# Filler products in two TensorE gaps of a router, fused attention logits, and a causal block left out

## The chip, the cores and the metric

The kernel runs on one core of a Trainium2 chip. The metric is device time in microseconds (us) of one execution, from start to end. TensorE (PE) does matrix products and transposes, VectorE (DVE) elementwise work and reductions, ScalarE (ACT) activations and copies, GpSimd (POOL) elementwise work in SBUF, and SyncE (SP) issues nearly all DMAs.

## The reference

A transformer stack on 256 tokens of width 1024, fp32 in and out. First a block with an indexed sparse attention, a spatial gating unit and a mixture of experts; then a two-layer stack with a windowed attention and a memory cross attention (layer 0), a gated linear recurrence with the same cross attention (layer 1) and a convolutional feed-forward in each. What the change touches:

```python
def dsa_attention(q, k, v, qi, ki, wi):          # 8 heads of 128
    ...                                           # 64 keys of each query are kept by an index score
    valid = sel <= qpos[None, :, None]            # causal
    logits = einsum('bqhd,bqkhd->bhqk', qb, kg) * (HEAD_DIM ** -0.5)
    logits = where(valid[:, None], logits, -inf)
    p = softmax(logits); out = p @ vg
...
def window_gqa_sink(q, k, v, sink):               # 16 heads of 64, keys within 128 positions
    m = maximum(max(s), sk)
    p = exp(s - m)
    p = p / (sum(p) + exp(sk - m))                # sk: one learned "sink" logit a head
...
def hier_moe(xn, ...):                            # 256 tokens, 4 groups of 8 experts
    g_sel = argmax(g_logits); top_v, top_i = top_k(e_in_group, 2)
    ...                                           # SwiGLU experts 1024 -> 2 x 256 -> 1024
```

## The kernel before, in words

Five engine programs are written out by hand and meet only through semaphores; each engine runs its program in order, so the order in the code is the order of the work. There is no scheduler.

**Linear layers.** Each weight matrix comes from HBM through a ring of SBUF slots, which SP refills when a slot has been used. ACT makes a rounded high part (L1428), POOL the remainder (L821), and PE multiplies high by high, low by high and high by low (L890 to L892, or L910 to L913 where the output is turned), in eight units of buffer.

**Attention** (three functions of this name, on PE, DVE and ACT). Tokens stand in two tiles of 128. A head goes through PE scores `sc_ps` (L964, four records a head), DVE logits `z_buf` = scores x scale + mask (L1879) and their row maximum `nmax` (L1883; with the sink L1886 and a small L1887), ACT exponentials with row sums (L1471), PE transposes of the probabilities (L975), an ACT copy of them to SBUF (L1489), PE products with the values (L995, eight records a head) and a DVE division (L1907). PE's order in iteration i is scores of head i+2, transposes of head i+1, values of head i; DVE's is the logits of head i+2, then the division of head i; ACT's is the copy of head i, then the exponentials of head i+2. Two score buffers and two probability buffers are used in turn. The first attention (`att`, 8 heads) is masked by the index and causally, the second (`att0`, 16 heads) has the window mask and the sink, and the memory attentions (`attx0`, `attx1`, 4 heads each) have no mask. The first two heads' scores are put ahead of the last part of the linear layer that stands before the attention.

**Router and experts.** The last linear layer of the first block's mixer (`w_out1`) is followed by transposes of its result (L1111), the router's logits (L1090) and a chain of some 25 small DVE operations that picks two experts a token (to L2114). PE then counts the tokens ahead of each one with triangular matrices (L1122), DVE turns that into places and a number of rounds (L2128 to L2132), and PE loads that number into a register. Eight batches of four experts follow: DVE makes selection matrices (L2144, L2146), PE gathers the tokens (L1131), DVE applies the gain (L2150), PE multiplies by the first expert weights (L1146) and the second (L1163) and scatters back (L1172). SP loads expert weights ahead into every slot that is free, and goes on to later batches as PE's semaphores report a slot used, first after the first half of batch 0's L1146.

## Time and profile before

| | |
|---|---|
| median of 3 runs | 1373.2 us (1373.08 to 1376.44) |
| the profiled execution, its own time | 1381.76 us |
| its span, first to last instruction | 1380.0 us, mean granted TensorE clock 0.975 |
| PE busy | 1254.0 us (91%) |
| POOL, ACT, DVE busy | 780.4, 634.9, 513.6 us |

Busy shares are averages over stages with different limits, so they don't say what a stage is worth. The chain that ended last does: it is followed back from the last instruction, at each step to what released it, and its shares are of the span. An interval between the starts of the same instruction in successive pairs of heads is the length of a cycle. Start-to-start distances are safer than durations on PE, whose records overlap.

### The profile page before, as it was taken

What the parts mean: (1) busy time and instruction counts of PE and PEld (TensorE: products, weight loads), DVE (VectorE), ACT (ScalarE), POOL (GpSimd) and SP (SyncE); (2) the same over time, 40 slices, a digit from 0 to 9 for tenths busy, and PEclk for the clock granted to TensorE, in tenths of its full rate; (3) what the DMA queues carried; (4) which work ended last, traced back from release to release, by engine and by line L of the source; (5) the groups of instructions that cost most, each with busy time, mean ns of one, the idle gap of its engine ahead of it and who ended that gap; (6) DMA issues with size and microseconds to landing.
All of it is one profiled execution on the core that took longest, in us unless ns stands there. A gap on an engine that the chain in (4) does not pass through costs nothing.

```text
span 1380.0 us, 19398 instructions
## 1 busy us (share of the span) xinstructions
PE 1254.0 (91%) x7815; PEld 1027.3 (74%) x7815; DVE 513.6 (37%) x1007; ACT 634.9 (46%) x1093; POOL 780.4 (57%) x347
## 2 busy tenths in 40 slices
PE   6999999897887877898889999999999889799997
PEld 5888877776333323777778999988998677799986
DVE  4629743443121111534733222202348281322211
ACT  5345534644011111644645555436698442655551
POOL 5769985440000000884017988878778904888884
PEclk9999999997999999998999999999999999899999
DMA  6645544276999999453005665445444523455552
GB/s 235 192 145 183 195 171 159 99 316 265 371 421 417 413 422 413 169 183 130 1 1 184 198 195 182 167 169 186 175 173 140 177 75 108 137 184 183 184 185 75
DMA packets 126116, 275.12 MB, mean 199 GB/s; under 512 B 7445, under 2 KB 53837, under 8 KB 113741
## 3 DMA queue, kind: packets, MB, share of 16 engines
q1 hardware_dynamic: 125328, 272.71, 54.2%
q8 instruction: 60, 0.98, 0.3%
q10 hardware_dynamic: 700, 1.21, 0.3%
q14 instruction: 28, 0.22, 0.1%
HBM read 272.85 MB, written 1.05 MB: 198 GB/s over the span
## 4 chain that ended last, share of the span: by engine, by line
PE 72%; DMA 9%; ACT 7%; DVE 6%; POOL 3%; issue 2%; ACTq 0%; SPq 0%; DVEq 0%
PE lin_ps L890 11%; PE lin_ps L892 11%; PE lin_ps L891 11%; PE lin_ps L910 8%; PE lin_ps L912 8%; PE lin_ps L913 8%; DMA ring<-in_w_expert_in 5%; POOL w_low L821 3%; PE sc_ps L1146 3%; DMA work<-in_w_expert_out 2%; ACT w_high L1428 2%; PE sc_ps L964 2%; PE lin_ps L995 1%; PE lin_ps L1163 1%; PE lin_ps L1131 1%
## 5 line engine op out<-in xcount | busy, mean ns | idle before, releaser
L821 POOL TENSOR_TENSOR w_low<-ring,w_high 128x1024 fp32r<-128x1024 f32 (+1 forms) x320 | 771.7, 2447 | 582.9 <-ACT w_high L1428 582.9
L1428 ACT ACTIVATE w_high<-ring 128x1024 fp32r<-128x1024 f32 (+1 forms) x320 | 312.2, 1040 | 136.9 <-PE lin_ps L892 88.8
L910 PE MATMUL lin_ps<-x_high,w_high 128*128 128x256 f32 x960 | 273.0, 284 | 0.0
L912 PE MATMUL lin_ps<-x_high,w_low 128*128 128x256 f32 x960 | 271.8, 283 | 0.0
L913 PE MATMUL lin_ps<-x_low,w_high 128*128 128x256 f32 x736 | 208.4, 283 | 0.0
L910 PEld LDWEIGHTS lin_ps<-x_high,w_high 128*128 128x128 f32 x960 | 184.5, 192 | 0.2
L912 PEld LDWEIGHTS lin_ps<-x_high,w_low 128*128 128x128 f32 x960 | 184.5, 192 | 0.1
L890 PE MATMUL lin_ps<-w_high,x_high 128*128 128x512 f32 (+1 forms) x432 | 170.9, 396 | 2.6 <-POOL w_low L821 2.6
L891 PE MATMUL lin_ps<-w_low,x_high 128*128 128x512 f32 (+1 forms) x432 | 168.8, 391 | 0.0
L892 PE MATMUL lin_ps<-w_high,x_low 128*128 128x512 f32 (+1 forms) x368 | 143.8, 391 | 0.0
L913 PEld LDWEIGHTS lin_ps<-x_low,w_high 128*128 128x128 f32 x736 | 141.5, 192 | 0.0
L890 PEld LDWEIGHTS lin_ps<-w_high,x_high 128*128 128x128 f32 x432 | 83.3, 193 | 20.2 <-issue 2.1
L891 PEld LDWEIGHTS lin_ps<-w_low,x_high 128*128 128x128 f32 x432 | 83.2, 193 | 16.2
L892 PEld LDWEIGHTS lin_ps<-w_high,x_low 128*128 128x128 f32 x368 | 70.8, 192 | 14.3
L1146 PE MATMUL sc_ps<-ring,work 128*32 128x512 f32 x496 | 59.9, 616 | 14.9 <-DMA ring<-in_w_expert_in 10.4
L1653 ACT ACTIVATE attn<-lin_ps,cols 128x256 f32<-128x256 f32 x44 | 18.5, 470 | 115.1 <-PE lin_ps L913 115.1
L890 PE MATMUL lin_ps<-w_high,hidden_high 128*128 128x512 f32 x176 | 68.5, 389 | 0.0
L891 PE MATMUL lin_ps<-w_low,hidden_high 128*128 128x512 f32 x176 | 68.5, 389 | 0.0
L892 PE MATMUL lin_ps<-w_high,hidden_low 128*128 128x512 f32 x176 | 68.5, 389 | 0.0
L2224 DVE SCALAR_TENSOR_TENSOR attn<-lin_ps,cols,attn 128x255 f32<-128x255 f32 x44 | 21.0, 478 | 126.2 <-ACT attn L1653 126.2
L913 PE MATMUL lin_ps<-u_low,w_high 128*128 128x256 f32 x224 | 63.4, 283 | 0.0
L1441 ACT ACTIVATE work<-lin_ps 128x1024 f32<-128x1024 f32 x20 | 20.5, 1026 | 83.6 <-PE lin_ps L892 83.6
(397 smaller groups left out, 1959.5 us busy)
## 6 DMA issues: line engine op xcount, KB each, us to landing
ring<-in_w_expert_in SPq DMA_DIRECT2D x31, 2048.0 KB, 14.4
ring<-in_ffn_w_in SPq DMA_DIRECT2D x44, 1024.0 KB, 7.6
ring<-in_w_in SPq DMA_DIRECT2D x14, 2048.0 KB, 7.8
ring<-in_b_w_in SPq DMA_DIRECT2D x11, 2048.0 KB, 8.0
work<-in_w_expert_out SPq DMA_DIRECT2D x8, 2048.0 KB, 23.9
ring<-in_w_expert_out SPq DMA_DIRECT2D x8, 2048.0 KB, 17.6
ring<-in_ffn_w_out SPq DMA_DIRECT2D x8, 2048.0 KB, 8.0
ring<-in_a_w_in SPq DMA_DIRECT2D x4, 2048.0 KB, 8.0
```

The costliest lines, as they stand in the source:

```text
L821: pool.tensor_tensor(w_low[:, slot, 0:words], raw, w_high[:, slot, 0:words].bitcast(F32), ALU.subtract).then_inc(low_made, 1)
L890: pe.matmul(out[:, t, :], high(k)[:, at], wh[:, j, :], start=(k == 0), stop=False)
L891: pe.matmul(out[:, t, :], high(k)[:, at], wl[:, j, :], start=False, stop=False)
L892: mm = pe.matmul(out[:, t, :], low(k)[:, at], wh[:, j, :], start=False, stop=(k == last_k))
L910: pe.matmul(out, wh[:, j, at], high(k), start=(k == 0 and f < 2), stop=False, skip_group_check=True)
L912: pe.matmul(out, wl[:, j, at], high(k), start=False, stop=False, skip_group_check=True)
L913: mm = pe.matmul(out, wh[:, j, at], low(k), start=False, stop=(k == last_k), skip_group_check=True)
L964: mm = pe.matmul(sc_ps[:, g % 2, SEQ * t:SEQ * (t + 1)], q(i, t), k(i), start=True, stop=True)
L1146: mm = pe.matmul(hid_ps[CAP * e:CAP * (e + 1), :], gathered[:, 4 * a + k, CAP * e:CAP * (e + 1)], extra_slot(e)[:, k, :] if extra and a == ...
L1428: act.activation(w_high[:, slot, 0:words], raw, ACT.Copy).then_inc(high_made, 1)
L1441: act.activation(dst, lin_out(name), func).then_inc(lin_moved[o % 2], 1)
L2224: step(dve.scalar_tensor_tensor(y[:, 1:SEQ], x[:, 0:SEQ - 1], col(f"conv{layer}", c), y[:, 1:SEQ], ALU.mult, ALU.add))
```

## The change

- **Router.** PE gets 34 products whose result nobody reads between the last router logits and the wait for the choice, and 14 more between the counting products and the wait that precedes the experts. Each has 128x128 weights and 256 columns out of `mem_high`, both operands in the rounded format, and writes to the bank pair that `w_out1` had used.
- **Fused logits.** In the two masked attentions, one fused DVE operation a token tile does (scores + mask) x (-scale) and the minimum over the row at the same time. The logits are kept with the sign turned, and ACT's exponential has scale -1. The sink enters as the starting value of the minimum, from a table `minus_sink` that one small DVE operation makes beforehand. A separate increment tells ACT that the minimum is there. In the attentions without a mask the two operations stay, with the sign turned.
- **Causal block.** In the first attention queries 0 to 127 can't see keys 128 to 255. That block is no longer computed: scores, logits and exponentials of tile 0 are 128 wide instead of 256, three blocks are transposed and copied instead of four, and three are multiplied by the values instead of four.

DVE in the second attention, from the logits of its head 2 to those of head 3 (`attn` holds logits, probabilities and masks, `sc_ps` the scores). Before:

```order
L1879 SCALAR_TENSOR_TENSOR attn<-sc_ps,attn 128x512 [waits att_probs,att_scores]
L1886 TENSOR_REDUCE nmax<-attn 128x2 [waits att_z]
L1887 TENSOR_SCALAR nmax<-nmax,sink 128x2 [waits dve_order]
L1902 TENSOR_TENSOR rsum<-rsum,esink 128x2 [waits att_sink,att_probs]
L1903 RECIPROCAL rsum<-rsum 128x2 [waits dve_order]
L1907 TENSOR_TENSOR work<-lin_ps,rsum 128x2x64 [waits att_out,dve_order]
L1879 SCALAR_TENSOR_TENSOR attn<-sc_ps,attn 128x512 [waits att_probs,att_scores]
```

and now:

```order
L1904 ISA attn,nmax<-sc_ps,attn,minus_sink 128x256 [waits att_z,att_probs,att_scores]
L1904 ISA nmax 128x1
L1904 ISA attn,nmax<-sc_ps,attn,minus_sink 128x256
L1904 ISA nmax 128x1
L1922 TENSOR_TENSOR rsum<-rsum,esink 128x2 [waits att_z,att_sink,att_probs]
L1923 RECIPROCAL rsum<-rsum 128x2 [waits dve_order]
L1927 TENSOR_TENSOR work<-lin_ps,rsum 128x2x64 [waits att_out,dve_order]
L1904 ISA attn,nmax<-sc_ps,attn,minus_sink 128x256 [waits att_probs,att_scores]
```

Three rows have become four: each fused operation has a second row that writes its accumulator, one number a row, to `nmax`.

PE at the router, from the last logits to the first gather (`route` tables are in `work`). Before:

```order
L1090 MATMUL lin_ps<-router_w,xT 128x36
L1122 MATMUL sc_ps<-work,before 128x32 [waits router_sel]
L1122 MATMUL sc_ps<-work,ones 128x32
L1122 MATMUL sc_ps<-work,before 128x32
L1122 MATMUL sc_ps<-work,ones 128x32 x2
L1182 TENSOR_LOAD rounds [waits router_done,normed]
L1182 ISA x2
L1131 MATMUL lin_ps<-work 128x128 [waits moe_pick]
```

and now:

```order
L1101 MATMUL lin_ps<-router_w,xT 128x36
L1131 MATMUL lin_ps<-mem_high 128x256 x34
L1139 MATMUL sc_ps<-work,before 128x32 [waits router_sel]
L1139 MATMUL sc_ps<-work,ones 128x32
L1139 MATMUL sc_ps<-work,before 128x32
L1139 MATMUL sc_ps<-work,ones 128x32 x2
L1131 MATMUL lin_ps<-mem_high 128x256 x14
L1200 TENSOR_LOAD rounds [waits router_done,normed]
L1200 ISA x2
L1149 MATMUL lin_ps<-work 128x128 [waits moe_pick]
```

The two groups of filler stand ahead of two waits; nothing else has moved on PE. On ACT the first attention's rows keep their order and get narrower.

```diff
@@ -75,6 +75,7 @@
 TINY = 1.0e-30
+FAR_UP = 3.0e38
 
@@ -284,6 +285,7 @@
         sink = sb("sink", [P, ATT_HEADS])
+        minus_sink = sb("minus_sink", [P, ATT_HEADS])
         post_sq = sb("post_sq", [P, 2, TILES])
@@ -450,6 +452,14 @@
 
+        def seen(tag):
+
+            return [(c, t) for c in range(TILES) for t in range(TILES) if P * c < keys_of(tag, t)]
+
+        def keys_of(tag, t):
+
+            return P if tag == "att" and t == 0 else SEQ
+
         att_bufs1 = tuple(work[:, 4096 + 1024 * i:4096 + 1024 * (i + 1)].rearrange("p (b t s) -> p b t s", b=2, t=TILES)
@@ -961,7 +971,8 @@
                     for t in range(TILES):
-                        mm = pe.matmul(sc_ps[:, g % 2, SEQ * t:SEQ * (t + 1)], q(i, t), k(i), start=True, stop=True)
+                        n = keys_of(tag, t)
+                        mm = pe.matmul(sc_ps[:, g % 2, SEQ * t:SEQ * t + n], q(i, t), k(i)[:, 0:n], start=True, stop=True)
                     mm.then_inc(att_scores, 1)
@@ -970,10 +981,8 @@
                         pe.wait_ge(tr_moved[k % 2], k // 2)
-                    for c in range(TILES):
-                        for t in range(TILES):
-                            mm = pe.transpose(tr_ps[:, k % 2, SEQ * c + P * t:SEQ * c + P * (t + 1)],
-                                              p_buf[:, g % 2, t, P * c:P * (c + 1)], ident[:])
+                    for n, (c, t) in enumerate(seen(tag)):
+                        mm = pe.transpose(tr_ps[:, k % 2, P * n:P * (n + 1)], p_buf[:, g % 2, t, P * c:P * (c + 1)], ident[:])
                     mm.then_inc(tr_done, 1)
@@ -990,10 +999,12 @@
                     out = small_out(pe, f"{tag}_{i}")
+                    pT = pT_buf[:, g % 2].rearrange("p c s -> p (c s)")
                     for t in range(TILES):
-                        for c in range(TILES):
-                            mm = pe.matmul(out[:, dim * t:dim * (t + 1)], pT_buf[:, g % 2, c, P * t:P * (t + 1)],
-                                           v(i, c), start=(c == 0), stop=(c == TILES - 1))
+                        chunks = [(c, n) for n, (c, of) in enumerate(seen(tag)) if of == t]
+                        for c, n in chunks:
+                            mm = pe.matmul(out[:, dim * t:dim * (t + 1)], pT[:, P * n:P * (n + 1)], v(i, c),
+                                           start=(c == 0), stop=(c == chunks[-1][0]))
                     mm.then_inc(att_out, 1)
@@ -1114,6 +1125,12 @@
             mm.then_inc(router_used, 1)
+
+            def keep_running(n):
+                for i in range(n):
+                    pe.matmul(lin_out("w_out1")[:, 0, 0:SEQ], mem_high[:, i % KC, 0:P], mem_high[:, i % KC, :], start=True, stop=True)
+
+            keep_running(34)
             pe.wait_ge(router_sel, 1)
@@ -1122,6 +1139,7 @@
             mm.then_inc(router_pos, 1)
+            keep_running(14)
             pe.wait_ge(normed, 3)
@@ -1468,7 +1486,8 @@
                     for t in range(TILES):
-                        ins = act.activation(p_buf[:, g % 2, t, :], z_buf[:, g % 2, t, :], ACT.Exp,
+                        n = keys_of(tag, t)
+                        ins = act.activation(p_buf[:, g % 2, t, 0:n], z_buf[:, g % 2, t, 0:n], ACT.Exp, scale=-1.0,
                                              bias=nmax[:, g % 4, t:t + 1], accum_out=rsum[:, g % 4, t:t + 1])
@@ -1486,7 +1505,8 @@
                     act.wait_ge(tr_done, k + 1)
-                    act.activation(pT_buf[:, g % 2], tr_ps[:, k % 2, :].rearrange("p (c s) -> p c s", c=TILES), ACT.Copy)\
+                    n = P * len(seen(tag))
+                    act.activation(pT_buf[:, g % 2].rearrange("p c s -> p (c s)")[:, 0:n], tr_ps[:, k % 2, 0:n], ACT.Copy)\
                         .then_inc(tr_moved[k % 2], 1)
@@ -1874,18 +1894,18 @@
                     if mask is None:
-                        ins = dve.tensor_scalar(z_buf[:, g % 2], s, scale, None, ALU.mult)
-                    else:
-                        ins = dve.scalar_tensor_tensor(z_buf[:, g % 2], s, scale, mask, ALU.mult, ALU.add)
+                        dve.tensor_scalar(z_buf[:, g % 2], s, -scale, None, ALU.mult).then_inc(att_z, 1)
+                        dve.wait_ge(att_z, g + 1)
+                        dve.tensor_reduce(nmax[:, g % 4, :], z_buf[:, g % 2], AX, ALU.min).then_inc(att_max, 1)
+                        return
+                    for t in range(TILES):
+                        lowest = minus_sink[:, i:i + 1] if with_sink else FAR_UP
+                        n = keys_of(tag, t)
+                        ins = dve.tensor_tensor_reduce(z_buf[:, g % 2, t, 0:n], s[:, t, 0:n], mask[:, t, 0:n], -scale, lowest,
+                                                       ALU.add, ALU.min, accum_out=nmax[:, g % 4, t:t + 1])
                     ins.then_inc(att_z, 1)
                     dve.wait_ge(att_z, g + 1)
-                    if not with_sink:
-                        dve.tensor_reduce(nmax[:, g % 4, :], z_buf[:, g % 2], AX, ALU.max, negate=True)\
-                            .then_inc(att_max, 1)
-                    else:
-                        step(dve.tensor_reduce(nmax[:, g % 4, :], z_buf[:, g % 2], AX, ALU.max))
-                        dve.tensor_scalar(nmax[:, g % 4, :], nmax[:, g % 4, :], sink[:, i:i + 1], -1.0, ALU.max,
-                                          ALU.mult).then_inc(att_max, 1)
+                    dve.sem_inc(att_max, 1)
 
@@ -2260,6 +2280,7 @@
                 dve.tensor_copy(k2_T[64:128, g, 1, :], tr_ps[64:128, k % 2, 0:SEQ]).then_inc(tr_moved[k % 2], 1)
+            step(dve.tensor_scalar(minus_sink[:], sink[:], -1.0, None, ALU.mult))
             dve.wait_ge(masks_made, 4)
```

## Rows read from the trace of the kernel before

**Rows 1.** The page, part 4: the chain that ended last, by engine.
```profile
PE 72%; DMA 9%; ACT 7%; DVE 6%; POOL 3%; issue 2%; ACTq 0%; SPq 0%; DVEq 0%
```
**Rows 2.** Stages: stretch, length, busy of five engines, clock, DMA share, GB/s.
```profile
652.82:680.80 27.98, 25.09 (x163) 20.37 (x163) 21.24 (x60) 17.64 (x62) 0.00 (x0) 1.00 0.07 27
...
646.87:652.82 5.95, 5.95 (x24) 5.48 (x25) 2.12 (x6) 2.02 (x8) 3.25 (x2) 0.51 0.20 53
...
323.40:339.20 15.80, 7.57 (x44) 7.17 (x45) 9.98 (x45) 9.61 (x16) 0.00 (x0) 0.66 0.98 397
...
339.20:348.00 8.80, 8.23 (x66) 5.30 (x68) 1.38 (x2) 1.67 (x2) 0.00 (x0) 0.83 0.02 6
...
348.00:547.00 199.00, 158.79 (x1030) 65.53 (x1022) 36.36 (x64) 24.87 (x43) 0.00 (x0) 0.98 1.01 416
...
328.50:342.10 13.60, 7.48 (x34) 7.35 (x35) 7.21 (x36) 5.14 (x8) 0.00 (x0) 0.50 0.79 333
```
**Rows 3.** Timeline, first attention, one cycle of two heads: start, us, engine, line.
```profile
247.72 1.03 PE L964 MATMUL sc_ps<-work 128*128 128x256 f32 x4
...
248.79 0.69 DVE L1879 SCALAR_TENSOR_TENSOR attn<-sc_ps,attn 128x512 f32<-128x512 f32 x1 [0.37 <-PE sc_ps L964]
...
249.51 0.69 DVE L1883 TENSOR_REDUCE nmax<-attn 128x2 f32<-128x512 f32 x1
...
250.23 0.51 ACT L1471 ACTIVATE attn<-attn,nmax 128x256 f32<-128x256 f32 x1 [1.37 <-DVE nmax L1883]
...
251.23 0.57 ACT L1489 ACTIVATE attn<-tr_ps 128x512 f32<-128x512 f32 x1
...
251.87 1.15 PE L995 MATMUL lin_ps<-work,attn 128*128 128x128 f32 x8
...
252.85 1.03 PE L964 MATMUL sc_ps<-work 128*128 128x256 f32 x4
```
**Rows 4.** Timeline, second attention, one cycle of two heads.
```profile
652.82 1.08 PE L964 MATMUL sc_ps<-work 128*128 128x256 f32 x4
...
653.94 0.69 DVE L1879 SCALAR_TENSOR_TENSOR attn<-sc_ps,attn 128x512 f32<-128x512 f32 x1 [0.56 <-PE sc_ps L964]
...
654.67 0.69 DVE L1886 TENSOR_REDUCE nmax<-attn 128x2 f32<-128x512 f32 x1
...
655.39 0.23 DVE L1887 TENSOR_SCALAR nmax<-nmax,sink 128x2 f32<-128x2 f32 x1
...
655.65 0.51 ACT L1471 ACTIVATE attn<-attn,nmax 128x256 f32<-128x256 f32 x1 [1.50 <-DVE nmax L1887]
...
656.79 0.66 PE L975 MATMUL tr_ps<-ident,attn 128*128 128x128 f32 x4 [0.57 <-ACT attn L1471]
...
658.40 1.08 PE L964 MATMUL sc_ps<-work 128*128 128x256 f32 x4
```
**Rows 5.** Groups by line and shape: count | busy us, mean ns | idle before.
```profile
L1862 DVE TENSOR_TENSOR attn<-work,attn 128x512 f32<-128x512 f32 x8 | 15.9, 1993 | 0.3
...
L1907 DVE TENSOR_TENSOR work<-lin_ps,rsum 128x128 f32<-128x128 f32 x16 | 4.7, 291 | 9.2 <-PE lin_ps L995 9.0
...
L634 DVE SCALAR_TENSOR_TENSOR x_low<-tr_ps,x_high 128x256 fp32r<-128x256 f32 x8 | 3.0, 420 | 3.3 <-ACT x_high L626 3.3
...
L1471 ACT ACTIVATION_READ_ACCUMULATOR attn<-attn,nmax 128x1 f32 x56 | 10.5, 187 | 0.0
```
**Rows 6.** The chain in order of time: start, us on the chain, what.
```profile
332.39 2.36 PE sc_ps L1122 x10
...
334.85 0.23 DVE work L2128
...
336.96 6.29 PE lin_ps L1131 x32
...
363.76 3.85 PE lin_ps L1131 x32
...
636.90 0.12 PE lin_ps L910
```

## The prediction

> **What bounds the kernel now.** I read the chain by engine first. TensorE holds 72% of it, DMA 9%, ACT 7% and DVE 6% [rows 1], so PE is the engine to watch, but the change takes work from DVE and ACT and adds some to PE. What it is worth depends on three places where PE is not the whole chain. I took those from the timeline, then from a table of stages.
>
> In the **first attention** a cycle of two heads lasts 5.13 us (scores at 247.72, again at 252.85). It goes once around: scores, logits at 248.79, maximum at 249.51, exponentials at 250.23, the copy of transposed probabilities at 251.23, values at 251.87, next scores [rows 3]. In the **second** a cycle is 5.58 us (652.82 to 658.40), and the same ring holds DVE's three operations from 653.94 to 655.65, after which PE stands 0.57 us for ACT [rows 4]. Five such cycles fill 652.82 to 680.80 (27.98 us) [rows 2]. A shorter step on DVE shortens both rings.
>
> At the **router** PE waits for the choice and counts at 332.39. The gather of the first expert batch takes 6.29 us where that of the second takes 3.85 [rows 6]. The granted clock explains the difference: it is 0.50 (1.2 GHz) from 328.5 to 342.1, after PE had run dry at the end of the router's narrow products, and later gathers run at 2.4 GHz [rows 2]. The **experts** are a DMA stage: from 348 to 547 the DMA share is 1.01 at 416 GB/s. A faster PE gains nothing inside. But DMA stands still (0.02, 6 GB/s) from 339.2 to 348.0, since every slot is full until PE has used half of batch 0's first weights [rows 2]. What PE gains before that point starts the stream earlier, and its end comes earlier by the same.
>
> **First attention.** The ring loses, per two heads:
> - scores: four records take about 0.88, 0.22 each; two become half as long: -0.22.
> - DVE: 248.79 to 250.23 is 1.44 [rows 3]. The fused operation isn't in the trace. Its nearest rows have the same operands, a PSUM and an SBUF tensor: 0.42 for 256 columns and 0.29 for 128 [rows 5]. Each has a second row that writes the accumulator. DVE has no such row before; ACT's takes 0.187 [rows 5], so it lies between 0 and 0.19, and I take 0.10. Hand-overs cost 0.03 (0.69 of work, 0.72 from start to start), and I put 0.04 on the separate increment. Sum 0.29 + 0.42 + 0.20 + 0.07 = 0.98: -0.46. The bounds for a pair are 0.74 (nothing beyond the work) and 1.44 (no gain).
> - ACT: exponentials and copy are each 128 columns narrower. A quarter of the copy's 0.57 would be 0.14; I take 0.10 for each: -0.20.
> - values: eight records in 0.98 (251.87 to 252.85) become six: -0.24.
>
> That is 1.12 a cycle, 4.01 left. PE's own work for two heads, 2 x (0.66 + 0.36 + 0.74) = 3.5, still fits under it, so PE doesn't take over. There are two full cycles: 2.24. Ahead of them two heads' scores (0.44) and one transpose (0.12) go out of PE's stream; the odd head follows 0.58 sooner (scores, transpose, values: PE alone); the end loses scores, DVE and exponentials once (0.78), a transpose (0.12) and the values of two heads (0.48). Less 0.22, because in the first cycle DVE is busy with another operation until the scores are there anyway: 4.5 us.
>
> **Second attention.** Nothing is left out here; only DVE changes. 1.71 (653.94 to 655.65) becomes 2 x 0.42 + 0.20 + 0.07 = 1.11: -0.60 a cycle. PE has 0.57 of idle and about 0.2 of waiting for the copy in each, so the ring stays the limit, barely (about 4.98 against 4.7 to 4.8). Five cycles give 3.0, the last head 0.6. From 646.87 to 652.82 PE is busy throughout at a clock of 0.51 [rows 2], so DVE gains nothing there; for the start, where ACT has other work queued, I take 0.3 between 0 and 0.6. Sum 3.9. The table `minus_sink` is made on 128x16 while DVE waits for scores: hidden; uncovered it would be one small operation, 0.23 like L1887 [rows 4].
>
> The Trainium skill speaks against fusing. VectorE: DVE Perf Modes, section The DRAIN you can't avoid, says that the next operation starts only when the pipe has emptied, and its Rules for kernel authors say not to fuse for speed but to lower the number of operations; that number goes up here, three to four and two to four. The trace agrees on the first half (0.69 long, 0.72 apart). By the rule the sum would be near no gain on DVE, which is the first rival below.
>
> **Router.** A product of 256 columns follows the last after 0.12 us at full clock [rows 6]. 34 take 4.1 and fit between 327.5 and 332.4; 14 take 1.7 and fit between the counting and 336.96. So with a full clock they delay nothing. But the clock can fall anyway: it fell 1.0 us after PE went idle, and the narrow products ahead are the same. In the trace it came back 5.1 us after PE resumed at 336.96. Counted from 327.5 that is 332.6; until then each product costs about twice 0.12, 0.22 with overlap, so 23 are done, and 11 more take 1.3, to 333.9. Counting at full clock takes 10 x 0.12 = 1.2, to 335.1, where it was 334.75: 0.35 late, DVE's L2128 waits for it [rows 6]. The second filler ends at 336.8. The gather then runs at full clock, 3.85 for 6.29: -2.44. I take -2.1. The bounds: never low, -2.6 (the 2.44 and the 0.1 to 0.2 by which counting is late now); low through all of it, 34 x 0.22 = 7.5 to 335.0, counting 2.36, and so on to a gather about 3.4 late that then runs fast, +1.0. The expert stream takes this over in full: its last load ahead ends at 339.2 [rows 2], and batch 0's products start at 344.0, 4.8 later, so they don't reach it. That burst begins after PE's last `w_out1` products and moves along with the first attention's gain.
>
> **Sum.** 4.5 + 2.1 + 3.9 = 10.5. The profiled execution would go from 1381.8 to 1371.3 (span 1380.0 to 1369.5). The median of the timed runs is 8.6 below the profiled one; the stages don't change with that, so 1373.2 - 10.5 = 1362.7.
>
> **Rivals.**
> - The fused operation saves nothing: the pipe empties four times, each accumulator row costs 0.3 to 0.4, and DVE's step stays 1.44 and 1.71. For it: the order shows the two extra rows. Against it: rows as small as L1887 cost 0.14 to 0.26 from start to start. Left are 4.5 less three times 0.46 (two cycles and the end), 3.1, and the router's 2.1, together 5.2: 1368.0. Chance 0.11.
> - The fillers don't hold the clock, or last into the wait for the number of rounds and delay it by as much as they give: router 0 to +1. Left are 8.4 or a little less: 1365. Chance 0.10.
> - More is gained: the clock also stays up at the second attention's start (PE's 5.95 us from 646.87 at half clock would take some 3), and an accumulator row is free (0.2 at each of nine places). 10.5 + 3 + 1.8 = 15.3: 1357.9. Chance 0.09.
> - Slower: the fused operation runs at half rate, and its accumulator row waits until the pipe is empty. There are DVE rows of that rate: L1862 takes 1993 ns for 512 columns, 1.0 for 256 [rows 5]; with 0.35 for the second row DVE's step is 2 x 1.35 + 0.07 = 2.77 in the second attention, +1.06 at six places (five cycles and the end), and 0.5 + 1.0 + 0.7 + 0.07 = 2.27 in the first, +0.83 at three. That is 8.9 against the 5.2 that is left elsewhere: 1376.9, on the other side. It decides from about 1.15 us for an operation of 256 columns with its second row. Against it: L1879 and L634 read one PSUM and one SBUF operand like the fused one and run at full rate, and the half rate stands in rows with two SBUF operands. Chance 0.04.
>
> The forecast has the remaining 0.66. Within it each 0.1 us of DVE's step moves the sum by 0.9 (nine places), and where the clock falls and rises by some 2, so its own range is 1359.5 to 1366. For 8 in 10 I take 1357.5 to 1368.5. A measurement tells 0.3% (4.1 us) from no change: faster is below 1369.1. That holds for the forecast, for the second and third rival and for a little over half of the first, whose 1368.0 lies near the bound: 0.66 + 0.10 + 0.09 + 0.06 = 0.91, rounded to 0.90. Same is the rest of the first and the mild end of the last, 0.07; slower 0.03.
>
> **What would show it.** Right: in the first attention scores of alternate heads about 4.0 apart, in the second about 5.0; a fused row of about 0.42 with a small row behind it; the first gather near 3.9 long; DMA's standstill before batch 0 about 6.7 instead of 8.8, and the experts' 199 us unchanged. Wrong: fused rows near 0.7, which keeps both cycles; fillers 0.21 apart to the end, with the counting behind them; or a DMA standstill that keeps its length because the loads ahead end later.

## The result: 10.6 us less

The kernel before took 1377.44 us at the median of 15 runs on this chip (1373.08 to 1382.45), the changed one 1366.27 us (1363.6 to 1371.25, 15 runs). The ratio is 0.9923 with the interval [0.9907, 0.9939]: 10.6 us less, 8.4 to 12.8. Here and below a ratio is to the kernel before as measured alongside; it is not the bare quotient of the two medians and differs from it by up to 0.25%. The forecast was 10.5 us less and 1362.7 us; the 3.6 us between 1362.7 and 1366.27 come almost wholly from the time it started at, 1373.2 of three runs, where fifteen give 1377.44. That the saving agrees to 0.1 us is partly luck: each of the three places saved more than forecast, 12.8 us in all in the profiled executions, and stages that the change leaves alone vary by some microseconds from one execution to the next. The profiled execution went from 1381.8 us (span 1380.0) to 1366.27 us (span 1364.5).

The page of the kernel after, engine shares of the chain that ended last (to [rows 1]):

```profile
PE 75%; DMA 7%; ACT 7%; DVE 5%; POOL 3%; issue 2%; ACTq 0%; SPq 0%; DVEq 0%
```

TensorE holds three points more, DVE one and DMA two less. In the timelines below a last row with a count under four only ends where the view ends.

**First attention.** The timeline of the kernel after, one cycle of two heads (start, us, engine, line; to [rows 3]):

```profile
246.23 0.82 PE L975 MATMUL sc_ps<-work 128*128 128x128 f32 x4
...
247.09 0.29 DVE L1904 CUSTOM_DVE_ANT_0 attn<-sc_ps,attn 128x128 f32<-128x128 f32 x1 [0.16 <-PE sc_ps L975]
...
247.31 0.08 DVE L1904 DVE_READ_ACCUMULATOR2_ANT nmax<- 128x1 f32 x1
247.31 0.42 DVE L1904 CUSTOM_DVE_ANT_0 attn<-sc_ps,attn 128x256 f32<-128x256 f32 x1
...
247.65 0.08 DVE L1904 DVE_READ_ACCUMULATOR2_ANT nmax<- 128x1 f32 x1
247.83 0.40 ACT L1490 ACTIVATE attn<-attn,nmax 128x128 f32<-128x128 f32 x1 [0.30 <-DVEq L1908]
...
250.01 0.60 PE L975 MATMUL sc_ps<-work 128*128 128x128 f32 x3
```

The fused operation on 128 columns takes 0.29 us, the one on 256 takes 0.42, and the exponentials start 0.74 us after the first of them, where it was 1.44. Scores of alternate heads are 250.01 - 246.23 = 3.78 us apart instead of 5.13.

**Second attention**, the same view (to [rows 4]):

```profile
642.46 1.08 PE L975 MATMUL sc_ps<-work 128*128 128x256 f32 x4
...
643.58 0.48 DVE L1904 CUSTOM_DVE_ANT_0 attn<-sc_ps,attn,minus_sink 128x256 f32<-128x256 f32 x1 [0.40 <-PE sc_ps L975]
643.99 0.08 DVE L1904 DVE_READ_ACCUMULATOR2_ANT nmax<- 128x1 f32 x1
643.99 0.48 DVE L1904 CUSTOM_DVE_ANT_0 attn<-sc_ps,attn,minus_sink 128x256 f32<-128x256 f32 x1
...
644.57 0.51 ACT L1490 ACTIVATE attn<-attn,nmax 128x256 f32<-128x256 f32 x1 [0.43 <-DVEq L1908]
...
647.32 0.43 PE L975 MATMUL sc_ps<-work 128*128 128x256 f32 x1
```

DVE's step is 644.57 - 643.58 = 0.99 us (1.71 before). The cycle is 647.32 - 642.46 = 4.86 us, 4.87 as the mean of five (5.58 before). The groups by shape (count | busy us, mean ns | idle before):

```profile
L1904 DVE CUSTOM_DVE_ANT_0 attn<-sc_ps,attn,minus_sink 128x256 f32<-128x256 f32 x32 | 14.2, 482 | 12.5 <-PE sc_ps L975 12.3 <-DVE nmax L1904 0.2
L1904 DVE DVE_READ_ACCUMULATOR2_ANT nmax<- 128x1 f32 x48 | 4.0, 84 | 0.0
L1904 DVE CUSTOM_DVE_ANT_0 attn<-sc_ps,attn 128x256 f32<-128x256 f32 x8 | 3.4, 420 | 0.0
```

**Stages** of the kernel after (stretch, length, busy of five engines, clock, DMA share, GB/s; to [rows 2]):

```profile
642.46:666.80 24.34, 24.29 (x163) 20.19 (x162) 15.17 (x70) 17.61 (x61) 0.00 (x0) 1.00 0.00 1
246.23:250.01 3.78, 3.62 (x29) 3.05 (x27) 2.47 (x13) 2.72 (x11) 0.00 (x0) 1.00 0.00 0
...
315.00:330.50 15.50, 12.02 (x98) 11.46 (x99) 10.26 (x45) 9.83 (x16) 0.00 (x0) 1.00 0.95 385
331.20:337.30 6.10, 5.53 (x54) 2.60 (x56) 0.94 (x2) 1.67 (x2) 0.00 (x0) 1.00 0.03 11
337.30:535.00 197.70, 157.78 (x1030) 65.32 (x1019) 36.39 (x64) 24.89 (x43) 0.00 (x0) 0.99 1.01 417
```

The first row is the five cycles that took 27.98 us. At the router the clock stays at 1.00 (it was 0.50 from 328.5 to 342.1). DMA stands still for 6.1 us instead of 8.8 ahead of the experts' stream, and the stream runs at 417 GB/s for 197.7 us (416 GB/s for 199.0 before). The chain at the router (start, us on the chain, what; to [rows 6]):

```profile
327.75 0.44 DVE work L2164
328.18 0.49 issue
328.67 3.85 PE lin_ps L1149 x32
```

The first gather takes 3.85 us instead of 6.29, as the second always did.

### The profile page after: what moved, and what is told of

It reads as the page before. It is cut to its first block, busy times and chain, and to the rows that moved or that the text cites. A ratio compares the mean times of both kernels' runs of the same rounds, so it can differ in the third digit from the quotient of the medians.

```text
span 1364.5 us, 19503 instructions
## 1 busy us (share of the span) xinstructions
PE 1249.6 (92%) x7839; PEld 1026.0 (75%) x7839; DVE 500.2 (37%) x1040; ACT 633.8 (46%) x1093; POOL 781.1 (57%) x347
## 4 chain that ended last, share of the span: by engine, by line
PE 75%; DMA 7%; ACT 7%; DVE 5%; POOL 3%; issue 2%; ACTq 0%; SPq 0%; DVEq 0%
PE lin_ps L900 12%; PE lin_ps L902 11%; PE lin_ps L901 11%; PE lin_ps L920 8%; PE lin_ps L922 8%; PE lin_ps L923 8%; DMA ring<-in_w_expert_in 4%; PE sc_ps L1164 3%; POOL w_low L831 3%; DMA work<-in_w_expert_out 2%; ACT w_high L1446 2%; PE lin_ps L1181 2%; PE lin_ps L1006 2%; PE sc_ps L975 2%; PE lin_ps L1149 1%
## 5 line engine op out<-in xcount | busy, mean ns | idle before, releaser
L1164 PE MATMUL sc_ps<-ring,work 128*32 128x512 f32 x496 | 58.9, 609 | 14.6 <-DMA ring<-in_w_expert_in 10.2
```

The source lines that it names most:

```text
L1164: mm = pe.matmul(hid_ps[CAP * e:CAP * (e + 1), :], gathered[:, 4 * a + k, CAP * e:CAP * (e + 1)], extra_slot(e)[:, k, :] if extra and a == ...
```

## The experiments

To compare executions I cut the profiled span at landmarks on PE: "first attention" from its first scores to the transposes of its result; "router" from the transposes of `h` to the first product of the experts (narrow products, choice, counting, gather); "experts" from there to the second half of the last batch's scatter; "second attention" from its first scores to those of the attention on the memory. In us, one profiled execution each:

| kernel | first attention | router | experts | second attention | span |
|---|---|---|---|---|---|
| before | 24.26 | 19.56 | 208.84 | 51.72 | 1380.0 |
| after | 19.20 | 16.96 | 207.31 | 46.61 | 1364.5 |
| after_again | 19.21 | 16.96 | 206.86 | 46.72 | 1363.6 |
| fill_only | 24.26 | 16.97 | 207.77 | 50.77 | 1371.4 |
| no_fill | 19.21 | 19.77 | 207.37 | 45.13 | 1365.6 |
| fused_only | 22.54 | 19.19 | 208.38 | 46.65 | 1370.8 |
| causal_only | 20.96 | 19.23 | 208.05 | 53.55 | 1376.6 |
| fill_first | 19.20 | 19.17 | 208.07 | 46.70 | 1367.6 |
| fill_second | 19.20 | 18.45 | 207.99 | 45.39 | 1362.9 |
| fill_long | 19.21 | 19.10 | 206.77 | 46.62 | 1368.1 |
| gap2 | 19.20 | 16.98 | 206.87 | 43.88 | 1364.3 |
| start_number | 19.21 | 16.95 | 206.99 | 44.31 | 1361.8 |
| gap3 | 19.21 | 16.96 | 207.94 | 46.67 | 1376.1 |
| gaps_number | 19.20 | 16.96 | 206.97 | 43.42 | 1371.3 |

The first attention repeats to 0.01 us. The second doesn't. It takes 45.13 to 46.72 us in the eight profiles whose program there is that of the kernel after, and 50.77 to 53.55 in the three with the old operations (before, fill_only, causal_only). One reason is a stretch at a granted clock of 0.50 near its start, which is longer in one execution than in another: 6.8 us from 633.7 in the kernel after, 3.4 us from 634.9 in start_number. Stages outside the table vary more: between the first attention and the router 59.7 to 64.0 us, between the experts and the second attention 80.4 to 87.2, and neither follows the edits.

### The parts alone

**fill_only**: the kernel before with both groups of unread products.

```
             mm.then_inc(router_used, 1)
+            keep_running(34)
             pe.wait_ge(router_sel, 1)
...
             mm.then_inc(router_pos, 1)
+            keep_running(14)
             pe.wait_ge(normed, 3)
```

> Only the 34 and 14 filler products are added to the kernel before; both attentions are untouched. Theory A (fillers keep TensorE at 2.4 GHz over the router, the first gather of experts falls from 6.3 to 3.9 us, and the DMA standstill ahead of batch 0 shortens by the same): about 2.5 us faster (ratio 0.998), first gather near 3.9 in the profile, distance from the start of that gather to the next product group 4.6 instead of 7.1. Theory B (in the two profiles the clock merely stood differently, and it falls anyway as often as not): gain under 1 us, a gather of 5 us or more in this profile.

Measured: 1378.26 us (1373.13 to 1381.47, 12 runs; before alongside 1380.96), ratio 0.9988 [0.9974, 1.0002]. The interval holds both no change and theory A's 2.5 us; the first gather takes 3.83 us in the profile, which is theory A.

**no_fill**: the kernel after without them.

```
-            keep_running(34)
...
-            keep_running(14)
```

> The changed kernel without both groups of fillers; fused logits and causal block stay. Theory A: the two attentions bring 5.1 + 5.1 = 10.2 us less what was clock luck, so 8 to 10 us faster than before, ratio 0.993 to 0.994; first attention from first scores to the next transposes 19.2 to 19.6, second from first scores to the memory attention's 46.6; the first gather back at 5.5 to 6.5 us. Theory B (attentions and fillers overlap in what they save, because the expert stage only takes one of them): the same time as the changed kernel within 1 us.

Measured: 1368.45 us (1365.97 to 1371.02, 6 runs), ratio 0.9921 [0.9898, 0.9944]. That is theory B's number, but not for its reason: the router stage is 2.8 us longer than in the kernel after and the experts' stage isn't shorter (207.37 for 207.31). The stage ahead of the second attention, where the programs are alike, is 2.6 us shorter.

**fused_only**: no_fill, and the causal block computed again.

```
         def keys_of(tag, t):
-            return P if tag == "att" and t == 0 else SEQ
+            return SEQ
```

> Fused logits in both masked attentions; the causal block is computed again, and there are no fillers. Theory A: the second attention keeps its whole gain, 4 to 5 us; the first has DVE's step at 2 x 0.42 + 0.17 + 0.07, about 1.0 instead of 1.44, at three places, 1.3 us; total 5.5 to 6.5 us faster, ratio 0.9955; cycle of two heads in the first attention 4.7. Rival: with full-width products TensorE is the limit of the first attention (2 x 2.3 = 4.7 of its own work), so its cycle stays above 4.9 and the gain there is under 0.7 us.

Measured: 1373.68 us (1370.94 to 1378.07, 12 runs), ratio 0.9958 [0.9941, 0.9976]. The cycle of the first attention is 4.56 us (246.01 to 250.57), so the theory holds and not the rival.

**causal_only**: no_fill with the logits and the maximum in separate operations, as in the kernel before; the upper right block stays out.

```
-                        ins = dve.tensor_tensor_reduce(z_buf[:, g % 2, t, 0:n], s[:, t, 0:n], mask[:, t, 0:n], -scale, lowest,
-                                                       ALU.add, ALU.min, accum_out=nmax[:, g % 4, t:t + 1])
+                        dve.scalar_tensor_tensor(z_buf[:, g % 2, 0, 0:P], s[:, 0, 0:P], scale, mask[:, 0, 0:P], ALU.mult, ALU.add)
+                        ins = dve.scalar_tensor_tensor(z_buf[:, g % 2, 1], s[:, 1], scale, mask[:, 1], ALU.mult, ALU.add)
...
+                        dve.tensor_reduce(nmax[:, g % 4, 0:1], z_buf[:, g % 2, 0:1, 0:P], AX, ALU.max, negate=True)
+                        dve.tensor_reduce(nmax[:, g % 4, 1:2], z_buf[:, g % 2, 1:2], AX, ALU.max, negate=True)\
+                            .then_inc(att_max, 1)
```

> Only the causal block of the first attention is left out: scores, exponentials, transposes, copy and values narrowed as in the changed kernel, but scaling with mask and maximum are two operations for each token tile, as wide as needed (128 and 256), with the sign as before; the second attention as before, no fillers. Theory A: ring 5.13 less 0.22 (scores), 0.24 (values), 0.20 (ScalarE), with VectorE's step about as long as before (2 x 0.29 + 2 x 0.42 + hand-overs = 1.5): cycle 4.5 to 4.6, total 2.5 to 3.5 us faster, ratio 0.998. Rival: four operations on VectorE instead of two make its step 1.6 or more and eat half of it: 1.5 us.

Measured: 1378.4 us (1373.94 to 1381.53, 12 runs), ratio 0.9986 [0.997, 1.0002]. DVE's step in the first attention is 1.30 us (247.42 to 248.72) and the cycle 4.35 (246.56 to 250.91).

What follows: in the first attention the two parts add. The causal block alone gives 24.26 - 20.96 = 3.30 us, the fused operation alone 24.26 - 22.54 = 1.72, both 5.05. In the second attention the gain is the fused operation's: 50.77 us or more in the three kernels without it, 46.72 or less in all that have it. The fillers show in the router stage. The seven kernels that have them as in the change take 16.95 to 16.98 us there, the four that have none 19.19 to 19.77; the first gather takes 3.8 us in the former and 5.9 to 6.5 in the latter, and in all eight profiles with both groups (fill_long among them) the granted clock stays at 1.00 through the router.

Taken by the times alone, only the fused operation is seen clearly, 0.42% or 5.8 us. The other two parts are worth 2 to 3.5 us, no more than what the placing of the low clock moves an execution by; fillers in (0.9923) and fillers out (0.9921) can't be told apart by time. That the fillers save 2.2 to 2.8 us is shown for their stage, and that the whole gets shorter by as much is not shown.

### What the fillers do

**fill_first** and **fill_second**: the kernel after with only the 34 products ahead of the choice, or only the 14 behind the counting (the other line taken out).

> The kernel after with the first group of 34 unread products alone; the second group of 14 is left out. Theory A: one busy stretch of PE is enough, the clock stays at 1.00 through the gather, which takes 3.85 us as in after. Theory B: the second gap alone is enough to bring the clock down, the gather's 32 products then run at 0.50 and take 6 to 6.5 us, 2.1 to 2.6 us more than in after. In the times, either is within what one execution differs from the next; the gather's row decides.

> The kernel after with the second group of 14 unread products alone; the first of 34 is left out. Theory: PE's idle in the first gap is what brings the clock down, so it falls as in the kernel without fillers, at about 324 to 327 us, and the gather takes near 6 us. Rival: work between the counting and the gather is enough for the gather to run at 1.00 (3.85 us), though the counting before it is slow.

Measured: fill_first 1371.13 us (1368.54 to 1372.28, 6 runs), ratio 0.9943 [0.9924, 0.9962]; fill_second 1364.63 us in its one run. The groups of PE from 322 to 340 us (count | busy us, mean ns | idle before), in fill_first:

```profile
L1148 PE MATMUL lin_ps<-work 128*128 128x128 f32 x32 | 6.0, 376 | 3.1 <-DVE work L2163 3.1
```

Its row of stages:

```profile
326.00:334.00 8.00, 5.16 (x26) 5.16 (x27) 3.12 (x11) 1.28 (x1) 0.00 (x0) 0.57 0.70 292
```

The same in fill_second:

```profile
L1148 PE MATMUL lin_ps<-work 128*128 128x128 f32 x32 | 4.5, 306 | 0.0
L1131 PE MATMUL lin_ps<-mem_high 128*128 128x256 f32 x14 | 3.3, 425 | 0.0
```

Its row of stages:

```profile
326.00:334.00 8.00, 5.38 (x25) 5.38 (x26) 5.42 (x28) 3.46 (x7) 0.00 (x0) 0.50 1.02 429
```

And in after_again, as in the kernel after:

```profile
L1149 PE MATMUL lin_ps<-work 128*128 128x128 f32 x32 | 3.8, 278 | 1.4 <-DVE work L2164 1.4
```

Its row of stages:

```profile
326.00:334.00 8.00, 6.06 (x55) 5.03 (x57) 3.42 (x10) 2.80 (x3) 0.00 (x0) 1.00 0.64 266
```

Theory B holds for fill_first: with the second gap open, PE stands from 325.7 us on for 3.1 us, the clock is 0.50 from 326.7 to 333.5, and the gather takes 6.0. In fill_second the clock has fallen (at 325.2) before its 14 products run; they take 3.3 us instead of 1.8 and end where the gather could start (no idle ahead of it), but it comes back during the gather, 4.5 us. So neither theory written for fill_second was quite right: both slow stretches exist, but the second is cut short. The router stage is 19.77 us with no fillers, 19.17 with the first, 18.45 with the second, 16.96 with both: 2.8 less with both. The first group alone gives nothing that can be told from the spread of the kernels without fillers (19.19 to 19.77), the second alone 0.7 to 1.3, in the one profile that each of them has. The two groups are one measure, since with either gap open the clock fell.

**fill_long**: 68 in place of 34.

```
-            keep_running(34)
+            keep_running(68)
```

> The kernel after with 68 instead of 34 unread products in the first gap of the router (14 in the second as before). In the profile after, 48 of them took 0.11 to 0.12 us each at the full clock, so 68 take about 8 us and end some 3 us after the choice has landed. Theory: the router's time passes through to the end whole, because the experts' stage follows at a fixed length (its transfers only start once the gather is done and then run at 417 GB/s). Then lead to gather grows by about 3 to 4 us, the experts' stage keeps its 207 us, and the whole is 3 to 4 us longer than after (ratio to before about 0.995). Rival: the experts' stage has slack of its own at its start, takes the delay up, and becomes shorter by as much. Of the clock both say the same: full through the router.

Measured: 1373.06 us (1369.86 to 1375.75, 9 runs), ratio 0.9957 [0.9942, 0.9972]. The chain there:

```profile
319.75 8.23 PE lin_ps L1131 x68
327.98 1.04 PE sc_ps L1139 x10
329.02 1.75 PE lin_ps L1131 x14
331.24 3.85 PE lin_ps L1149 x32
```

The fillers stand in the chain themselves now. The router stage is 19.10 - 16.96 = 2.14 us longer, less than the 3 to 4 expected, because PE's idle ahead of the counting (0.80 us in the kernel after) is gone and that ahead of the gather falls from 1.36 to 0.47. The experts' 206.77 lies beside after_again's 206.86: the delay passes through whole, which is what the prediction needed to count the router's gain in full. The whole became 4.7 us longer (0.9957 less 0.9923, intervals 1.5 thousandths wide on each side; 6.7 against the 0.9908 of after_again), more than the 2.1; of the 3.6 us by which its span is longer 1.85 stand in the linear stage ahead of the second attention, where the kernels are alike.

### The second attention's start and its limit

**gap2**: 22 more unread products in PE's idle ahead of the second attention's first products with the values.

```
                         turn_probs(i + 1)
+                    if tag == "att0" and i == 0:
+                        at = blocks["att0_0"][0] % 2
+                        for n in range(22):
+                            pe.matmul(lin_ps[:, 2 * at + 1, 0:SEQ], mem_high[:, n % KC, 0:P], mem_high[:, n % KC, :],
+                                      start=True, stop=True)
                     pe.wait_ge(tr_moved[job % 2], job // 2 + 1)
```

> The kernel after with 22 more unread products in PE's idle 2.7 us ahead of the second attention's first products with the values, at the granted clock of that place about 0.11 to 0.22 us each. In after the clock there was 0.50 until 638.5 us and the first products of the second attention took from 633.93 to 642.46, 8.5 us. Theory: it was PE's standstill that brought the clock down, so with it filled the stretch runs at 1.00 and is 2 to 2.6 us shorter, and the whole is shorter by that (ratio to before about 0.990). Rival: the clock falls there anyway, since the linear attention ahead of it keeps PE idle in other places too; then the fillers run at half clock, 22 of them take 4.8 us instead of 2.4, and the second attention starts about 2 us later than in after (ratio about 0.994).

Measured: 1365.64 us (1364.77 to 1367.56, 6 runs), ratio 0.9905 [0.9887, 0.9923]. PE's timeline in the kernel after, from the gap on:

```profile
633.93 1.97 PE L1006 MATMUL lin_ps<-work,attn 128*128 128x64 f32 x8 [2.66 <-ACT attn L1509]
...
642.46 0.87 PE L975 MATMUL sc_ps<-work 128*128 128x256 f32 x3
```

and in gap2:

```profile
634.27 2.88 PE L1003 MATMUL lin_ps<-mem_high 128*128 128x256 f32 x22
637.17 1.10 PE L1011 MATMUL lin_ps<-work,attn 128*128 128x64 f32 x8
...
642.98 1.08 PE L975 MATMUL sc_ps<-work 128*128 128x256 f32 x4
```

The stretch from 634 to 640 as a row of stages, first in the kernel after, then in gap2:

```profile
634.00:640.00 6.00, 6.00 (x25) 5.53 (x25) 1.52 (x7) 2.79 (x12) 3.18 (x2) 0.50 0.22 61
```

```profile
634.00:640.00 6.00, 5.97 (x49) 5.62 (x47) 2.28 (x10) 4.77 (x10) 4.23 (x2) 1.00 0.28 110
```

In the kernel after the low stretch runs from 633.7 to 640.6, not to the 638.5 that the expectation names. The theory holds: the values' first products still start 7.99 us after the first scores (637.17 - 629.18; in the kernel after 633.93 - 625.94), so the fillers delay nothing, and the way to the third following scores falls from 8.53 us to 642.98 - 637.17 = 5.81. That is 2.7 us of the stage (46.61 to 43.88), and 1.3 us less than the shortest execution without these fillers (no_fill, 45.13), whose low stretch is 3.4 us long. The ratio points the same way, but its interval overlaps that of the kernel after (0.9908 [0.9881, 0.9936] in a repeat).

**start_number**: the constant as start value of the minimum, so the sink isn't in the maximum that is subtracted.

```
-                        lowest = minus_sink[:, i:i + 1] if with_sink else FAR_UP
+                        lowest = FAR_UP
```

> The kernel after with the constant 3.0e38 in place of each row's minus sink as the start value of the fused minimum in the second attention; it leaves the sink out of the maximum that is subtracted. Theory: the pointer to a start value is what makes a 128x256 row 482 ns there and 420 ns in the first attention, so the 32 rows become 420 ns and the VectorE step of a head falls from 0.99 to about 0.87 us. The cycle of the second attention stays at 4.87 us, because PE is busy 24.29 of 24.34 us there, and the time stays as in after. Rival: the step still ends last at some heads, and the attention becomes shorter by up to 0.12 us a head, 2 us in all.

Measured: 1364.13 us (1362.52 to 1370.97, 6 runs), ratio 0.9909 [0.9883, 0.9935]. The timeline of one head in start_number:

```profile
647.42 0.42 DVE L1904 CUSTOM_DVE_ANT_0 attn<-sc_ps,attn 128x256 f32<-128x256 f32 x1 [0.56 <-PE sc_ps L975]
...
647.76 0.42 DVE L1904 CUSTOM_DVE_ANT_0 attn<-sc_ps,attn 128x256 f32<-128x256 f32 x1
...
648.28 0.51 ACT L1490 ACTIVATE attn<-attn,nmax 128x256 f32<-128x256 f32 x1 [0.52 <-DVEq L1908]
```

The five cycles, as a row of stages:

```profile
641.55:665.27 23.72, 23.70 (x162) 20.33 (x162) 13.95 (x70) 17.60 (x61) 0.00 (x0) 1.00 0.03 13
```

The start value that is read per partition is what costs 61 ns a row (482 against 421 here), and the step is 0.86 us. But the cycle went to 23.72 / 5 = 4.74 us from 4.87, by just what the step lost, and that is the rival. I had read "PE busy 24.29 of 24.34" as PE being the limit; here it is busy 23.70 of 23.72 in a shorter cycle with the same products. The ring through DVE and ACT is still the limit after the change, and a busy share close to 1 didn't show otherwise. The gain is 0.6 us; the other 1.7 of this stage's 2.3 go with the low clock at its start, 3.4 us long here and 6.8 in the kernel after. The times can't show 0.6 us: 0.9909 stands beside after_again's 0.9908.

### Two that were to be better still

**after_again** is the kernel after as it is. **gap3** adds 64 unread products where I took PE's idle of 8.7 us near 1157 us to be:

```
             linear("kv11", *from_mem)
+            o = blocks["b10"][0]
+            pe.wait_ge(lin_moved[o % 2], o // 2)
+            for n in range(64):
+                pe.matmul(lin_ps[:, 2 * (o % 2), 0:SEQ], mem_high[:, n % KC, 0:P], mem_high[:, n % KC, :], start=True, stop=True)
             pe.wait_ge(normed, 9)
```

**gaps_number** has the edits of gap2, gap3 and start_number.

> The kernel after once more, on the same chip as the three beside it, as the measure for them. Its ratio to before was 0.9923 [0.9907, 0.9939]; expected again within that. Its profile shows which low stretches of the clock stay in their place and which come and go: theory, those at the router stay away and the one behind 631 us and the one of 10.2 us behind 1157 us are there again; rival, the clock's falls shift at random and some of what was put down to the fillers is luck.

> The kernel after with 64 unread products where PE stands for 8.7 us ahead of the transposes of the second cross stage's input, near 1157 us. In every profile so far the clock was 0.50 for 10.2 us from that stretch on, and the transposes and first products behind it took about 4.6 us at half clock. Theory: filled, the clock stays at 1.00 and those 4.6 us take about 2.5, so the whole is some 2.1 us shorter than after; the 64 products take 7.7 us and end 1 us ahead of the wait's end. Rival: the transposes behind it are held up by VectorE, not by PE's clock, and nothing is gained.

> The kernel after with the filler at the second attention's start, the filler near 1157 us, and the constant start value in the second attention (the sink left out of the maximum that is subtracted). Expected if they add: 2.7 (second attention's start, as gap2 showed) + 2.1 + 0.6 (cycle 4.74 instead of 4.87 us, as start_number showed) = 5.4 us less than after, ratio to before about 0.988. Rival: the clock's falls move elsewhere once these places are filled, and the whole gains 3 us or less.

Measured: after_again 1366.02 us (1359.32 to 1368.65, 6 runs), ratio 0.9908 [0.9881, 0.9936]; gap3 1375.03 us (median of 12; eleven from 1373.21 to 1377.86 and a single one of 4358.3 that nothing here explains), ratio 0.9971 [0.9956, 0.9986]; gaps_number 1370.78 us (1369.69 to 1373.11, 6 runs), ratio 0.9946 [0.9925, 0.9967]. The timeline of gap3:

```profile
940.71 7.83 PE L1279 MATMUL lin_ps<-mem_high 128*128 128x256 f32 x64
...
948.38 0.60 PE L948 MATMUL tr_ps<-ident,work 128*128 128x128 f32 x4
```

Both missed, and the reason is plain: the line I chose stands at 940 us, not at 1157. There the wait behind it had long been met and PE had no idle, so the fillers delayed everything by their 7.7 us. The gap near 1157 (8.7 us from 1155.0 in after_again) belongs to a later norm and was never filled; whether its 10.2 us of low clock can be had back is open. The run does give the price of a filler without a gap: all of it. gap2 with start_number alone, without the misplaced part, wasn't run. Inside the second attention, which the misplaced part doesn't touch, the two do add: the stage is 43.42 us in gaps_number against 46.72 in after_again, 3.3 less for an expected 2.7 + 0.6.

after_again shows which low stretches hold their place: none at the router, one of 6.8 us from 633.5 and one of 10.2 from 1159.1, as in the kernel after.

## Why the prediction was right, and where its sizes were off

**The mechanism** was right in all three places, and each part's stage showed it; for the router the stage alone shows it. Of the 15.5 us between the two spans the three stages hold 5.06 + 2.60 + 5.11 = 12.8. The other 2.7 stand in stages that the change leaves alone: 1.5, 1.6 and 1.5 us less ahead of the first attention, between it and the router, and in the experts' stage, 0.4 and 1.5 us more ahead of and behind the second attention. Between the first attention and the router the clock is 0.50 for 6.8 us in the profile of before and for 3.4 us in that of after; the others are not explained. The medians differ by 11.2, the ratio gives 10.6, and the forecast sum was 10.5. Each term was put too low, and the agreement of the sum with the measured time owes something to luck.

**First attention, 4.5 forecast, 5.06 measured.** The cycle was 3.78 instead of 4.01. The mis-sized term is DVE's step, 0.74 for a forecast 0.98. Its operations have the durations taken from [rows 5], 0.29 and 0.42. The accumulator row, put at 0.10 each, is 84 ns long but runs beside the start of the next operation (both at 247.31), so the first of the two costs nothing. And the second fused operation starts 0.22 us after the first, which is 0.29 long: with no wait between them they overlap by 0.07. The step came out at the lower bound of 0.74 that the prediction gave, though not by its sum: it is 0.22 to the second operation, 0.42 for that, and 0.10 until ACT starts.

**The page against fusing.** The trace shows overlap between operations that don't wait for each other, and DVE's steps fell to 0.74 and 0.99 us where a gain of nothing would have left 1.44 and 1.71. The Trainium skill (VectorE: DVE Perf Modes, section The DRAIN you can't avoid) says that one can't skip the emptying of the pipe by chaining operations without semaphores. The trace doesn't agree with that here, nor with the advice not to fuse in that page's Rules for kernel authors: alone the fusion was worth 5.8 us. The Trainium skill (same page, section Two Vector instructions with no wait between them) gives a model in which such an instruction is held back only where start quadrants (groups of 32 partitions) differ. Here all operands start at partition 0, and with that model the trace agrees. The pair that the prediction took as agreement, 0.69 long and 0.72 apart, has a wait between its two operations. The trace of before had a pair of which neither waits for the other: L1887 starts at 640.42, takes 0.23, and the next logits start at 640.55. Nor is the overlap a matter of fusing: in causal_only plain operations of 0.29 have the next one 0.21 behind them (247.42, 247.63).

**Second attention, 3.9 forecast, 5.11 measured.** The cycle, 4.87 for 4.98, is 0.1 better, although the fused row is 0.48 and not 0.42: what was lost on the pointer was won on the accumulator row and the overlap (0.99 for 1.11). A row of before could have told the 0.48. It has the same line and operands as the 0.42 of [rows 5], and beside them an operand `cols` that is read per partition, as `minus_sink` is:

```profile
L634 DVE SCALAR_TENSOR_TENSOR x_low<-tr_ps,cols,x_high 128x256 fp32r<-128x256 f32 x16 | 7.1, 479 | 13.9 <-ACT x_high L626 13.9
```

The term that was mis-sized most is the start, put at 0.3 between 0 and 0.6: the way from the first scores to the first values is 7.99 us (625.94 to 633.93) where it was 9.05 (637.82 to 646.87), so 1.06. The timeline of this place in before:

```profile
638.97 0.69 DVE L1879 SCALAR_TENSOR_TENSOR attn<-sc_ps,attn 128x512 f32<-128x512 f32 x1 [3.97 <-PE sc_ps L964]
...
640.68 0.51 ACT L1471 ACTIVATE attn<-attn,nmax 128x256 f32<-128x256 f32 x1 [10.18 <-DVE nmax L1887]
...
642.26 0.51 ACT L1471 ACTIVATE attn<-attn,nmax 128x256 f32<-128x256 f32 x1 [0.30 <-DVE nmax L1887]
...
646.24 0.58 ACT L1489 ACTIVATE attn<-tr_ps 128x512 f32<-128x512 f32 x1
```

and in after:

```profile
627.16 0.48 DVE L1904 CUSTOM_DVE_ANT_0 attn<-sc_ps,attn,minus_sink 128x256 f32<-128x256 f32 x1 [3.17 <-PE sc_ps L975]
...
628.15 0.51 ACT L1490 ACTIVATE attn<-attn,nmax 128x256 f32<-128x256 f32 x1 [9.55 <-DVEq L1908]
...
629.33 0.49 ACT L1490 ACTIVATE attn<-attn,nmax 128x256 f32<-128x256 f32 x1
...
633.30 0.58 ACT L1509 ACTIVATE attn<-tr_ps 128x512 f32<-128x512 f32 x1
```

The first head's exponentials start 0.99 us after its logits instead of 1.71, and the second head's start 1.18 after the first's instead of 1.58, since ACT no longer waits for DVE there; the logits themselves start 0.07 later behind the first scores. From there to the copy it is 3.98 and 3.97 us: the other work in ACT's queue stands behind these exponentials, in order, and moves along with them. The prediction took it as cover for the gain, and it was none.

**Router, 2.1 forecast, 2.60 measured.** I had the clock fall and come back; it never fell, the bound of -2.6. fill_second comes nearest to the case of the forecast's working: there the clock falls, the 14 fillers take 3.3 us, and it comes back in the gather. That a change of the router stage reaches the experts' stage whole is shown by fill_long.

**The rivals.** "The fused operation saves nothing" fell with fused_only (5.8 us). "The fillers give nothing" fell in the profile, and can't be decided by the times. "More is gained" was half right: the first of the two accumulator rows was free, but the clock did fall at the second attention's start, and gap2 shows what holding it would give, 2.7 us for the 3 that it put there. Of "slower" nothing came: the fused operation takes the 0.42 and 0.29 us of the plain one on the same operands. The row named there for half rate, L1862, is slower than that: 1993 ns where L1879 takes 0.69 us for the same 512 columns.

## What to carry to other kernels

A reduction fused into the operation that makes its input takes most of the second operation out of a ring in which DVE is a link (1.44 us to 0.87 in fused_only): take its duration from a row with the same operands, one that is read per partition included, and count neither the accumulator row nor the operation behind it in full if nothing waits between them. Fillers held the clock here only with both gaps filled. They cost every microsecond of themselves where PE isn't idle, and have to be placed by the time at which their line runs, not by its look in the program. To find out whether PE limits a ring, shorten the other link and see whether the cycle follows; its busy share was 0.998 before and 0.999 after that, while the cycle shrank.

## What the runs showed of the hardware that I had not expected

- A start value of the fused minimum that is read per partition makes a 128x256 row 482 ns instead of 420 (421 in start_number).
- Two fused DVE operations with no wait between them start 0.22 us apart when the first is 0.29 long, 0.41 when it is 0.48, and 0.34 when it is 0.42: 0.07 to 0.08 less than its length each time.
- The accumulator read of DVE is 84 ns, against 187 for ACT's [rows 5], and has the same start as the next fused operation.
- With either of the router's two gaps left open the granted clock fell to 0.50: in fill_first PE stood 3.1 us in the second and the gather took 6.0 us.
